# Two tiles per transfer for the rows of the PE convolution, three quarters of them issued by GpSimd

## The reference

```python
def conformer_conv(h, w1, b1, dw, dwb, ln_g, ln_b, w2, b2):
    u = h @ w1 + b1
    a, g = jnp.split(u, 2, axis=-1)
    u = a * jax.nn.sigmoid(g)
    u = dwconv(u, dw) + dwb          # depthwise, 31 taps along the tokens
    u = jax.nn.silu(layernorm(u, ln_g, ln_b))
    return u @ w2 + b2
```

## Time and profile before

| | |
|---|---|
| median of 3 runs | 3214.43 us (3210.39 to 3217.61) |
| the profiled execution, its own time | 3211.2 us |
| its span, first to last instruction | 3209.0 us |
| PE busy | 3007.0 us (94%) |
| DVE busy | 1545.2 us (48%) |
| ACT busy | 1197.5 us (37%) |
| POOL busy | 214.5 us (7%) |
| mean granted TensorE clock | 0.973 of full speed |

### The profile page before, as it was taken

How to read it: one execution, slowest core, us unless ns; L and a number is a source line. 1 busy time by engine, 2 the same in 40 slices (tenths; PEclk the granted TensorE clock), 3 DMA queues, 4 the chain that set the end, 5 groups by cost and what they waited for, 6 DMA issues and landing times.

```text
span 3209.0 us, 42156 instructions
## 1 busy us (share of the span) xinstructions
PE 3007.0 (94%) x17944; PEld 2500.2 (78%) x17944; DVE 1545.2 (48%) x2477; ACT 1197.5 (37%) x1939; POOL 214.5 (7%) x282
## 2 busy tenths in 40 slices
PE   8998999989999989999767799999999999998898
PEld 7987898879977757888543378888787888787898
DVE  6664554755445445444411254443545444444565
ACT  5443443654444434222211243222324323343443
POOL 0000000000013210000000000000000000134100
PEclk9999999999999999999978899999999999999999
DMA  6555666567655443232353533333333332266454
GB/s 227 186 167 188 230 228 222 176 225 231 198 140 79 66 138 117 92 102 95 118 176 109 174 118 118 118 118 128 108 98 113 99 99 92 79 115 103 111 184 132
DMA packets 350747, 450.78 MB, mean 140 GB/s; under 512 B 11840, under 2 KB 331616, under 8 KB 338272
## 3 DMA queue, kind: packets, MB, share of 16 engines
q1 hardware_dynamic: 346032, 438.06, 41.8%
q0 software_dynamic: 4368, 9.45, 4.5%
q10 hardware_dynamic: 160, 0.59, 0.0%
HBM read 437.63 MB, written 1.05 MB: 137 GB/s over the span
## 4 chain that ended last, share of the span: by engine, by line
PE 83%; DVE 7%; ACT 4%; SPq 3%; DMA 2%; issue 1%; POOL 0%; DVEq 0%; ACTq 0%
PE ps L1052 24%; PE ps L1054 23%; PE ps L1053 23%; SPq L1025 2%; PE ps L1094 2%; PE ps L1233 2%; PE ps L1073 1%; DVE lo L1545 1%; PE ps L1075 1%; PE ps L1074 1%; DVE lo L1548 1%; PE ps L1224 1%; ACT hi L1266 1%; DMA raw<-in_mod_w 1%; PE ps L1085 1%
## 5 line engine op out<-in xcount | busy, mean ns | idle before, releaser
L1052 PE MATMUL ps<-XN,hi 128*128 128x256 f32 (+1 forms) x3008 | 1020.9, 339 | 45.0 <-DVE XN L1571 21.0
L1053 PE MATMUL ps<-XN,hi 128*128 128x256 f32 (+1 forms) x3008 | 1003.1, 333 | 0.0
L1054 PE MATMUL ps<-XN,lo 128*128 128x256 f32 (+1 forms) x3008 | 1002.6, 333 | 0.0
L1052 PEld LDWEIGHTS ps<-XN,hi 128*128 128x128 f32 x3008 | 578.7, 192 | 161.8 <-DVE XN L1571 35.6
L1545 DVE TENSOR_TENSOR lo<-raw,hi 128x1024 fp32r<-128x1024 f32 (+1 forms) x313 | 385.4, 1231 | 532.6 <-ACT hi L1266 514.3
L1054 PEld LDWEIGHTS ps<-XN,lo 128*128 128x128 f32 x3008 | 578.5, 192 | 54.5
L1053 PEld LDWEIGHTS ps<-XN,hi 128*128 128x128 f32 x3008 | 579.0, 192 | 51.2
L1266 ACT ACTIVATE hi<-raw 128x1024 fp32r<-128x1024 f32 (+1 forms) x313 | 326.9, 1044 | 510.3 <-PE ps L1054 430.0
L1548 DVE TENSOR_TENSOR lo<-raw,hi 128x1024 fp32r<-128x1024 f32 (+1 forms) x313 | 381.9, 1220 | 0.0
L1052 PE MATMUL ps<-H,hi 128*128 128x512 f32 (+1 forms) x1024 | 371.3, 363 | 0.0
L1053 PE MATMUL ps<-H,hi 128*128 128x512 f32 (+1 forms) x1024 | 371.2, 363 | 0.0
(11 more groups left out here) (230 smaller groups left out, 3294.8 us busy)
## 6 DMA issues: line engine op xcount, KB each, us to landing
raw<-in_mlp_w SPq DMA_DIRECT2D x128, 1024.0 KB, 5.3
raw<-in_mod_w SPq DMA_DIRECT2D x96, 1024.0 KB, 4.9
raw<-in_ffn_w_in SPq DMA_DIRECT2D x44, 1024.0 KB, 5.4
raw<-in_attn_w_in SPq DMA_DIRECT2D x36, 1024.0 KB, 5.4
raw<-in_na_wqkv SPq DMA_DIRECT2D x24, 1024.0 KB, 5.2
raw<-in_ffn_w_out SPq DMA_DIRECT2D x16, 1024.0 KB, 5.3
raw<-in_mlstm_w_in SPq DMA_DIRECT2D x12, 1024.0 KB, 5.4
raw<-in_cv_w SPq DMA_DIRECT2D x12, 1024.0 KB, 6.5
```

Of the source, the lines that this page charges most:

```text
L1052: e.matmul(out, whi, xhi, start=first, stop=False)
L1053: e.matmul(out, whi, xlo, start=False, stop=False)
L1054: i = e.matmul(out, wlo, xhi, start=False, stop=last)
```

## The change

The spread is made once for each chunk, after its second tile, and one DMA carries both tiles: 16 DMAs of 32 rows x 2 x 572 values for a chunk. SP and GpSimd share them by the group g of 32 features. For the chunks 0 to 2 GpSimd issues the groups 0 to 2 (12 DMAs) and SP group 3 (4 DMAs); for chunk 3 each issues two groups (8 DMAs). `UX` has two buffers of two tiles in place of three of one (4 tile buffers in place of 3). `SGM` has one buffer in place of two, so the sigmoid of tile k waits until VectorE has used that of tile k-2. The semaphores are one for each issuing engine and buffer (`uxs0`, `uxs1`, `uxp0`, `uxp1`).

```diff
-        ("U", [P, 4, 576], F32), ("UX", [P, 3, 4, 576], F32), ("WD", [P, 2, 4, 8, 32], F32),
-        ("CV", [P, KT, 512], F32), ("AB", [P, 2, 512], F32), ("SGM", [P, 2, 2, 512], F32))
+        ("U", [P, 4, 576], F32), ("UX", [P, 2, 4, 2, 576], F32), ("WD", [P, 2, 4, 8, 32], F32),
+        ("CV", [P, KT, 512], F32), ("AB", [P, 2, 512], F32), ("SGM", [P, 2, 512], F32))
...
         def evac_a(t, b, u):
             p.do("cv_a", 2 * c + t, t, b, u)
-            p.do("cv_spread", 2 * c + t)
+            if t == 1:
+                p.do("cv_spread", c, 3 if c < 3 else 2)
...
+def spread(e, m, c, g, signal, name):
+
+    for i in range(4):
+        e.dma_start(m.UX[32 * i:32 * i + 32, c % 2, g, :, 0:572],
+                    m.U[32 * g:32 * g + 32, 2 * (c % 2):2 * (c % 2) + 2, i:i + 572]).then_inc(*signal.says((name, c)))
...
 def sync(e, w, m, p, T, sig):
-    def cv_spread(k):
-
-        w.wait_ge(("cv_u", k), ("conv", k - 3) if k >= 3 else None)
-        for g in range(4):
-            for i in range(4):
-                e.dma_start(m.UX[32 * i:32 * i + 32, k % 3, g, 0:572],
-                            m.U[32 * g:32 * g + 32, k % 4, i:i + 572]).then_inc(
-                    *sig[f"ux{k % 3}"].says(("ux", k)))
+    def cv_spread(c, g0):
+        w.wait_ge(("cv_u", 2 * c + 1), ("conv", 2 * c - 3) if c >= 2 else None)
+        for g in range(g0, 4):
+            spread(e, m, c, g, sig[f"uxs{c % 2}"], "ux_sp")
...
     def cv_conv(k, b, u):
-        w.wait_ge(("ux", k), ("wd", k), free_of(b, u))
+        w.wait_ge(("ux_sp", k // 2), ("ux_pool", k // 2), ("wd", k), free_of(b, u))
...
     def cv_g(c, t, b, u):
-        w.wait_ge(("acc", b, u), ("cv_u", k - 4) if c >= 2 else None)
+        w.wait_ge(("acc", b, u), ("cv_u", k - 2) if c else None)
...
     def cv_a(k, t, b, u):
-        w.wait_ge(("acc", b, u), ("cv_s", k), "cv_pads", ("ux", k - 4) if k >= 4 else None)
+        w.wait_ge(("acc", b, u), ("cv_s", k), "cv_pads")
+        if k >= 4:
+            w.wait_ge(("ux_sp", k // 2 - 2), ("ux_pool", k // 2 - 2))
...
 def gpsimd(e, w, m, p, T, sig):
+    def cv_spread(c, g0):
+        w.wait_ge(("cv_u", 2 * c + 1), ("conv", 2 * c - 3) if c >= 2 else None)
+        for g in range(g0):
+            spread(e, m, c, g, sig[f"uxp{c % 2}"], "ux_pool")
```

More of the change, by code:

```diff
@@ L149, in allocate @@
     m.sem = {n: ctx.enter_context(nc.semaphore(f"s_{n}"))
-             for n in ["acc", "act", "high", "dve", "low", "pool", "ld", "x0", "x1", "taps", "ux0", "ux1", "ux2", "pv", "ci", "pos", "cst", "tb0", "tb1", "out"]
+             for n in ["acc", "act", "high", "dve", "low", "pool", "ld", "x0", "x1", "taps", "uxs0", "uxs1", "uxp0", "uxp1", "pv", "ci", "pos", "cst", "tb0", "tb1", "out"]
              + [f"raw{i}" for i in range(RAW)]}
@@ L1228, in cv_conv @@
     def cv_conv(k, b, u):
-        w.wait_ge(("ux", k), ("wd", k), free_of(b, u))
+        w.wait_ge(("ux_sp", k // 2), ("ux_pool", k // 2), ("wd", k), free_of(b, u))
         for j in range(8):
             for g in range(4):
-                rows = m.UX[:, k % 3, g, :].rearrange("p (s t) -> p s t", s=2)
+                rows = m.UX[:, k // 2 % 2, g, k % 2, :].rearrange("p (s t) -> p s t", s=2)
                 f = e.matmul(m.ps[b][32 * g:32 * g + 32, :], m.WD[:, k % 2, g, j, :], rows[:, :, 4 * j:4 * j + S],
@@ L1467, in cv_g @@
         k = 2 * c + t
-        w.wait_ge(("acc", b, u), ("cv_u", k - 4) if c >= 2 else None)
-        e.activation(m.SGM[:, c % 2, t, :], m.ps[b][:, :], ACT.Sigmoid, bias=param(m, "cv_b1_2", k, 1)).then_inc(
+        w.wait_ge(("acc", b, u), ("cv_u", k - 2) if c else None)
+        e.activation(m.SGM[:, t, :], m.ps[b][:, :], ACT.Sigmoid, bias=param(m, "cv_b1_2", k, 1)).then_inc(
             *act.says(("free", b, u), ("cv_s", k)))
@@ L1844, in cv_a @@
             in0=m.ps[b].rearrange("p (s t) -> p s t", s=2), scalar=param(m, "cv_b1_2", k),
-            in1=m.SGM[:, k // 2 % 2, t, :].rearrange("p (s t) -> p s t", s=2), op0=ALU.add, op1=ALU.mult).then_inc(
+            in1=m.SGM[:, t, :].rearrange("p (s t) -> p s t", s=2), op0=ALU.add, op1=ALU.mult).then_inc(
             *dve.says(("free", b, u), ("cv_u", k)))
@@ L1980, in gpsimd @@
     go_through(p, {"square": square, "context": context, "ml_pads": ml_pads, "na_zero": na_zero,
-                   "na_table": na_table, "cv_pads": cv_pads, "sc_pads": sc_pads})
+                   "na_table": na_table, "cv_pads": cv_pads, "cv_spread": cv_spread, "sc_pads": sc_pads})
 def signals(m, table):
```

## The result

| | before | after |
|---|---|---|
| median | 3214.97 us (4 runs, 3210.39 to 3217.61) | 3192.85 us (4 runs, 3191.59 to 3197.25) |
| ratio, 95% interval | | 0.9935 [0.9918, 0.9952] |
| the profiled execution | 3211.2 us | 3197.25 us |
| convolution stage, from the modulation matmul at the end of chunk 0's value half to the one behind the layer norm's sums | 1587.05 to 1829.06: 242.0 us | 1592.38 to 1813.48: 221.1 us |
| the three stalls ahead of `mod_w` | 62.35 us | 42.64 us |

The kernel became 22.1 us faster; 31 us were forecast. The profiled execution of after was the slowest of its four runs, and it comes 5.3 us later to this stage, which the change does not touch before it. Read inside the stage, the two traces differ by 20.9 us.

What follows compares the result with a forecast made beforehand. The prediction took SP's queue order, which stalls TensorE ahead of `mod_w` loads, as the bound. 3211.2 - 30.9 (chunks 0 to 2) - 0.6 (chunk 3) = 3179.7, plus 3.2 for the median: 3182.9, forecast 3183 us; range 3171 to 3197.

Steps and rivals of the forecast that it cites:

- What bounded the kernel: Convolution stage: SP issues a chunk's 32 row DMAs ahead of the `mod_w` load; three TensorE stalls, 62.35 us in all.
- The lower bound of the stall: Chunks 0 to 2: if the load lands undisturbed 5.33 us after its issue, TensorE stands still 7.7 us.
- The load's delay beside GpSimd's rows: Chunks 0 to 2: GpSimd's transfers in flight beside the `mod_w` load add 2.8 us to the stall.
- X: The stall left ahead of `mod_w` in each of chunks 0 to 2: forecast 10.5 us, bounds 7.7 and 15.5.
- rival (b): Chunks 0 to 2: the load lands after most of `UX`, stall 14 to 15.5 us, 3197 us; chance 0.16 with (d).
- the case that I forecast: Chunks 0 to 2: stalls of 9 to 13 us, giving 3175 to 3190 us; chance 0.56.
- (d): TensorE waits at the queue's next load; each stall gives back some 3 us, 3192 us; chance 0.16 with rival (b).
- One of my own signs of being wrong: SP's queue: the load behind 4 DMAs landing later than 10 us would show the prediction wrong.
- the worst case: Chunks 0 to 2: the load goes last and lands at 1669.7, upper bound of the stall given as 15.5 us.
- The slow clock: TensorE's granted clock of 0.50 during and after each stall stays; cost nothing, 1 us a stall in the range.
- GpSimd's DMAs and UX in time: Chunks 0 to 2: GpSimd's DMAs take 0.62 us each to issue, rows land before the convolution needs them; cost 0.
- Chunk 3: Last chunk: `UX` 3.6 us later, 4.2 us given back from `mod_w` waits and clock; 0.6 us saved.

Runs made afterwards that it cites:

- experiment 7: The kernel before, with only SP's 32 one-tile transfers of chunks 0 to 2 moved behind the next two weight loads: 3145.49 us, 0.9785.
- experiment 1: The change, but GpSimd's twelve row transfers of chunks 0 to 2 start only when the `mod_w` load has landed: 3196.12 us, 0.9932 of the kernel before.
- experiment 3: The change, but GpSimd issues all 16 transfers of chunks 0 to 2 and SP none there: 3181.85 us, 0.9891 of the kernel before.
- experiment 9: The change, but all four copies of a group start at value 0, without the shift by tokens: one run, 3191.14 us.

## Why the prediction was right, and where it was off

**What bounded the kernel: right.** The queue's order, not the data, made the three stalls: experiment 7 moves nothing but the order, and the stalls are gone.

**The lower bound of the stall: right.** 7.7 us was worked out, 7.97, 7.72 and 7.81 were measured with GpSimd out of the way (experiment 1).

**The load's delay beside GpSimd's rows: the term that was mis-sized.** I took 2.8 us, "near to the row" of the neighbourhood attention. It measured 14.2 - 7.8 = 6.4 us; three times the difference is 11 us, which is the miss (30.9 forecast for these chunks, 19.7 measured). I chose the nearest row although my own work with the engines' time, half for each queue, gave 4 us and an X of 11.7: a group of `TB` transfers is 3 us of work and ends, while GpSimd's rows were 7.3 us of work by my sum. And even the half share was too small. SP's queue had 52.0% of 11.7 us, or 6.1 us, for 1.62 MB: its last rows, the load, and some 0.1 MB of the load behind it. My sum had 5.0 us for all four rows and the load, 1.64 MB, because it counted the load at 401 GB/s, a rate of several loads together. The rows were sized right: q0 moved 1.38 MB in 50.1% of 11.7 us, 235 GB/s, against 240.

The round robin of the Trainium skill ("DMA: Bandwidth & Descriptors", "Queues, rings and completion order") goes packet by packet; I had turned it into equal time, which gave 11.7. As far as the profile's packets are those of the page, the trace agrees with the rule but not with my use of it: from 1662 to 1664 us each queue had 114 packets, for which GpSimd's took 75.9% of the time and SP's 29.9%. Which packets met in these 11.7 us, and how much of the 6.4 us that explains, no run settles.

**What came out is rival (b), and not the case that I forecast.** A mean stall of 14.2 us lies outside my 9 to 13 and inside the 14 to 15.5 of (b), and the 19.7 us saved lie in its 16 to 20. Its mechanism fits too, in the main: the engines were full, and when the load had landed at 1664.2, GpSimd's queue had moved 1.53 of its 1.76 MB. Only the load's bytes were not held to the end, since from 1658 to 1660 us SP's queue had 80.2% of the time. One of my own signs of being wrong also came: the load behind the four transfers landed 11.6 us after its issue, and I had set 10. The time lies in my range because the range was drawn out to (b), to which (with (d)) I had given 0.16. The prediction also has a slip: its own terms for the worst case, 1669.7 - 1653.85, give 15.9 us and not 15.5.

**The slow clock: right.** The granted clock is 0.50 in the window inside chunk 1's stall and 0.53 in the one behind it, about as before, and the stage changed by 20.9 us, of which the stalls are 19.7.

```profile
1656.00:1660.00 4.00, 0.00 (x0) 0.00 (x0) 0.00 (x0) 0.00 (x0) 0.63 (x2) 0.50 1.03 276
...
1665.00:1670.00 5.00, 5.00 (x18) 3.11 (x11) 0.00 (x0) 0.60 (x1) 0.00 (x0) 0.53 1.07 338
```

**GpSimd's DMAs and UX in time: right.** They took 0.54 us each (0.62 forecast), and there was no wait for `UX` in the chunks 0 to 2.

**Chunk 3: right.** Forecast 0.6 us saved and a wait for `UX` of about 10 us; measured 11.21 us, and from the modulation matmuls ahead of it to the last of the sums 34.5 us (1761.57 to 1796.04) for 34.9 before (1776.88 to 1811.79), 0.4 us saved.

**What I did not ask** is what the experiments found: the load that TensorE stalls for could have stood ahead of the rows all along. I priced the queue as the change left it, and the remaining 14 us looked like a cost of bandwidth. They were still a cost of order.

## What to carry to other kernels

When a queue issues both transfers that must wait for a result and loads whose buffer is already free, put the loads first: that alone was worth three times the change that shortened the issue and moved it to another engine. Before a transfer is handed to a second queue, add up the work of everything that will then be in flight; while the load was in flight each of the two queues had half of the full engines' time on average, and in shorter stretches between 13% and 80%. Twice the work of the load and of all that stands ahead of it in its queue was too low an estimate here: 10 us by my sum, where 14.2 us went by from the first row's issue (1649.99) to the load's landing. And hold back the loads that nobody needs yet: in experiment 3 they took half of the time from the rows.

## What the runs showed of the hardware that I had not expected

- A GpSimd DMA of 64 pieces of 2288 bytes takes 0.54 us to issue, one of 256 pieces of 256 bytes 0.62.
- Beside full engines the issue of a 1 MB load on SP took 1.36 us in place of 0.58, and with GpSimd's rows held back (experiment 1) 0.59 again, so the collision lengthened the queue too.
- Rows from SBUF to SBUF mixed with loads moved at about 255 GB/s with a DMA share of 1.0 (256 in the change, 255 in experiment 3), where loads alone reached 401; the alignment of a row's start made no difference (experiment 9).
